# The last two layers of a fused two-network kernel: attention by head pairs with GEMMs between its tiles, norms from column sums, two products split into parts

## The chip, the cores and the metric
The kernel runs on one core of a Trainium2 chip. The metric is device time in microseconds (us) of one execution; lower is better. The engines are TensorE (PE; PEld is its weight load), VectorE (DVE), ScalarE (ACT), GpSimd (POOL) and SyncE (SP), which here only issues DMAs. They run at once and meet at semaphores; each takes its own instructions in order.

## The reference
The program computes two networks in a row on 512 tokens of width 1024. The first (two layers, mixer and mixture of experts) is not touched. The second, also two layers, is:

```python
def second_block(x, norm1_g, w_in, q_norm_g, k_norm_g, sg_norm_g, sg_w, sg_b, conv_w,
              w_out, norm2_g, ffn_w_up, ffn_conv_w, ffn_w_down):
    ...
    for l in range(DEPTH):                                   # DEPTH = 2
        h = _rmsnorm(x, norm1_g[l])
        p = h @ w_in[l]                                      # 1024 x 2048
        q, k, v, su, sv, cb, cc, cx = jnp.split(p, split_at, axis=-1)
        q = _axial_rope(_rmsnorm(q.reshape(b, s, 8, 64), q_norm_g[l]), tabs)
        k = _axial_rope(_rmsnorm(k.reshape(b, s, 2, 64), k_norm_g[l]), tabs)
        a_out = _block_attention(q, k, v.reshape(b, s, 2, 64))   # softmax, 4 query heads per key head
        g_out = _spatial_gating(su, sv, sg_norm_g[l], sg_w[l], sg_b[l])
        c_out = cb * _dwconv3(cc * cx, conv_w[l])
        mix = jnp.concatenate([a_out, g_out, c_out], axis=-1)
        x = x + mix @ w_out[l]                               # 1024 x 1024
        h2 = _rmsnorm(x, norm2_g[l])
        up = _dwconv3(h2 @ ffn_w_up[l], ffn_conv_w[l])       # 1024 x 5632
        gate, val = jnp.split(up, 2, axis=-1)
        x = x + (jax.nn.silu(gate) * val) @ ffn_w_down[l]    # 2816 x 1024
    return x
```

(In the quoted loop norm and rope of q and of k are drawn together into one line each.)

## The kernel before
Everything is fp32 and feature-major: a [128 features, 512 tokens] tile is one PSUM bank, and xT and hT hold eight of them. A "ticket" (TB, from order_b) is one tile that TensorE makes in one bank; tickets go round the eight banks in the order of the list, the second entry names the engine that frees the bank ("V" VectorE, "A" ScalarE), and TensorE opens a bank when the ticket eight places earlier is freed. So one list sets TensorE's order and the banks.

A product in fp32 streams its moving operand several times (two records a matmul in the trace). The gate, value and up products are instead "split": weights and rows are each a rounded high part in fp32r plus a low part, and a tile is the sum of three one-pass terms, high x high, low weights x high rows, high weights x low rows (of_parts, 24 matmuls of 512 columns for a contraction of 1024). The high part of a weight block is a ScalarE copy (high_part(n), into ring slot 4 or 5), the low part a POOL subtraction in place (low_part(n), L798), one block of 128x4096 ahead of TensorE. SP loads weight blocks into ring slots in the order of blocks_b; a block waits for the last reader of its slot. The output product (wo, 8 tiles, contraction 1024) and the second feed-forward product (dn, 8 tiles, contraction 2816 = 22 x 128) are plain fp32.

A layer: whole_norm("n1") squares x on ScalarE, sums with eight ones-matmuls 512 columns wide, so that the sum stands in all 128 partitions, takes a root (ScalarE) and a reciprocal (VectorE) over 128x512, scales xT into hT (L1808, one instruction per 128 features), and makes high (ScalarE) and low parts (L1812). Then the tiles q, kk, v, k, su, sv, cb, cc, cx, with a head norm of the same kind (nr, halves-matmul, root, reciprocal, L1826) for each of six q and k tiles, and rope (sw, swap-matmul, three VectorE instructions, L1831 to L1833). Then gating and convolution. Attention runs head by head over 8 heads x 4 query tiles: logits (L, a matmul with 64 rows), maximum and its negation (L1880, L1881), exponential with sum (L2212), reciprocal and multiplication (L1885, L1886), four transposes (T, L1320), copies to bwT (L1875 or L1915), and after four tiles the values (pv, four matmuls of 64 columns). Then wo, the second norm n2, 44 up tiles (ug, uv), and dn.

Line 819 is the helper mm, through which nearly every matmul goes; line 1915 is the ScalarE copy helper and 685 POOL's helper for small DMAs.

## Time and profile before

| | us |
|---|---|
| median of 3 runs | 3931.11 (3924.7 to 3931.31) |
| profiled execution | 3928.03 |
| its span | 3926.4 |
| mean granted TensorE clock | 0.917 of full |
| TensorE busy | 3308.7 |
| VectorE, ScalarE, POOL busy | 1194.5, 863.4, 669.9 |
| first network and set-up | 2449.6 |
| first layer of the second network | 734.0 |
| second layer and output | 742.8 |

Times in the trace count from the span's start. A busy figure is the sum of instruction records; TensorE's records overlap a little at their ends, so a stage that is full shows a busy time equal to its length. PEclk is the clock that the throttle granted TensorE: 1.0 is 2.4 GHz and 0.5 is 1.2 GHz. Stages are named A to G in the text: A first norm with its first two tiles, B the rest up to attention, C attention, D output product, E second norm with its first two tiles, F the other 42 up tiles, G second feed-forward product.

### The profile page before, as it was taken

The numbers are of one execution on the slowest core, as the hardware profiler recorded it, in microseconds if no ns is written. First come the engines' busy times: TensorE is split into PE (matmuls) and PEld (weight loads), VectorE is DVE, ScalarE is ACT, GpSimd is POOL, SyncE is SP. The second block draws the span as 40 slices with busy tenths as digits, with TensorE's granted clock in tenths as the row PEclk, the third lists the DMA queues.
The fourth block names the chain that finished last, engine by engine and source line by source line (L and its number), as shares of the span: only waits on it lengthen the run. The fifth ranks groups of instructions, "written<-read, shape, count | busy, mean of one in ns | idle before, by whom it ended". The sixth has DMA issues, their size and how long they took to land. (4 is left out here: it accounts for less than half of the span.)

```text
span 3926.4 us, 41122 instructions
## 1 busy us (share of the span) xinstructions
PE 3308.7 (84%) x14327; PEld 1938.3 (49%) x14327; DVE 1194.5 (30%) x2137; ACT 863.4 (22%) x1257; POOL 669.9 (17%) x360
## 2 busy tenths in 40 slices
PE   6976997888784985898888875889799989879999
PEld 4753564333322763564333332743587456338854
DVE  4564213111103465312211111452433016433310
ACT  4333111111112423201111111222332022323300
POOL 4220000111112311010111113200343030013300
PEclk8987997999996997898899997989899998889999
DMA  5124132999994114133899997110223311012322
GB/s 198 65 95 139 54 141 96 406 409 409 409 393 172 65 59 154 65 101 137 326 408 409 409 407 287 60 38 22 65 86 88 106 66 65 1 43 86 101 59 66
DMA packets 287657, 663.59 MB, mean 169 GB/s; under 512 B 20190, under 2 KB 110612, under 8 KB 287504
## 3 DMA queue, kind: packets, MB, share of 16 engines
q1 hardware_dynamic: 269632, 623.43, 42.8%
q0 software_dynamic: 17872, 38.14, 2.7%
q8 instruction: 93, 1.52, 0.2%
q14 instruction: 60, 0.49, 0.0%
HBM read 653.64 MB, written 25.69 MB: 173 GB/s over the span
## 5 line engine op out<-in xcount | busy, mean ns | idle before, releaser
L819 PE MATMUL psum<-s_parts 128*128 128x512 f32 (+3 forms) x3392 | 823.5, 396 | 114.5 <-ACT s_parts L1915 96.7
L819 PE MATMUL psum<-s_ring,s_units 128*64 128x512 f32 x3168 | 743.9, 619 | 135.6 <-DMA s_ring<-in_w_expert_in 96.5
L819 PEld LDWEIGHTS psum<-s_parts 128*128 128x128 f32 (+1 forms) x3392 | 632.6, 192 | 277.0 <-issue 103.2
L819 PEld LDWEIGHTS psum<-s_ring,s_units 128*64 128x64 f32 x3168 | 247.5, 141 | 588.3 <-issue 445.8
L819 PE MATMUL psum<-s_units,s_ring 128*128 128x512 f32 x1216 | 524.0, 592 | 3.3 <-DVE s_units L1588 3.3
L819 PE MATMUL psum<-s_units 128*128 (+9 forms) x1544 | 404.9, 441 | 111.3 <-ACT s_units L1915 51.3
L798 POOL TENSOR_TENSOR s_parts<-s_ring,s_parts 128x4096 fp32r<-128x4096 f32 x30 | 270.4, 9019 | 988.6 <-ACT s_parts L1915 988.6
L819 PEld LDWEIGHTS psum<-s_units,s_ring 128*128 128x128 f32 x1216 | 230.8, 190 | 290.9 <-issue 290.1
L819 PE MATMUL psum<-s_h_low,s_parts 128*128 128x512 f32 (+1 forms) x1440 | 355.7, 389 | 0.0
L819 PEld LDWEIGHTS psum<-s_units 64*128 64x128 f32 (+3 forms) x1544 | 207.2, 203 | 238.3 <-issue 188.9
L819 PEld LDWEIGHTS psum<-s_h_low,s_parts 128*128 128x128 f32 (+1 forms) x1440 | 269.0, 187 | 57.4
L707 POOL TENSOR_TENSOR s_parts<-s_ring,s_parts 128x4096 fp32r<-128x4096 f32 (+1 forms) x22 | 180.5, 8209 | 596.3 <-ACT s_parts L1915 596.3
L1704 DVE TENSOR_SCALAR s_put_at<-psum,s_half_row 128x1 int32<-128x1 f32 x66 | 14.4, 218 | 706.9 <-DMA ys_scratch<-s_units,s_put_at 706.9
L1915 ACT ACTIVATE s_parts<-s_ring 128x4096 fp32r<-128x4096 f32 (+1 forms) x52 | 181.3, 3493 | 197.2 <-DMA s_ring<-in_w_in 197.2
L1915 ACT ACTIVATE s_units<-psum 128x512 f32<-128x512 f32 (+1 forms) x246 | 143.2, 598 | 285.7 <-PE psum L819 236.9
L749 POOL DMA_INDIRECT s_units<-h_scratch,s_take_at x66 | 82.9, 1256 | 597.3 <-DVE s_take_at L1699 477.5
L1899 DVE SCALAR_TENSOR_TENSOR s_units<-psum,s_par,s_units 128x511 f32<-128x511 f32 x88 | 66.0, 750 | 301.2 <-ACT s_units L2239 301.2
L2239 ACT ACTIVATE s_units<-psum,s_par 128x512 f32<-128x512 f32 x88 | 60.8, 690 | 335.5 <-PE psum L819 335.5
L1398 DVE RECIPROCAL s_temps<-s_temps 128x512 f32<-128x512 f32 x36 | 120.7, 3353 | 25.1 <-ACT s_temps L1940 25.1
L2116 ACT ACTIVATE s_units<-psum,s_gsl 128x512 f32<-128x512 f32 x66 | 45.4, 687 | 358.7 <-PE psum L819 358.7
L758 POOL DMA_INDIRECT ys_scratch<-s_units,s_put_at x66 | 67.1, 1016 | 321.2 <-ACT s_units L2116 286.5
L819 PE MATMUL psum<-s_hT,s_ring 128*128 128x512 f32 x256 | 110.4, 593 | 1.7 <-ACT s_hT L1915 1.7
(306 smaller groups left out, 2407.1 us busy)
## 6 DMA issues: line engine op xcount, KB each, us to landing
s_ring<-in_w_expert_in SPq DMA_DIRECT2D x132, 2048.0 KB, 23.9
s_ring<-in_w_expert_out SPq DMA_DIRECT2D x66, 2048.0 KB, 24.9
s_ring<-in_w_in SPq DMA_DIRECT2D x28, 2048.0 KB, 8.0
s_ring<-in_w_ada SPq DMA_DIRECT2D x24, 2048.0 KB, 8.1
s_ring<-in_ffn_w_up SPq DMA_DIRECT2D x44, 1024.0 KB, 6.9
s_ring<-in_ffn_w_down SPq DMA_DIRECT2D x16, 1408.0 KB, 7.1
s_ring<-in_w_out SPq DMA_DIRECT2D x8, 2048.0 KB, 7.8
s_units<-ys_scratch POOLq DMA_DIRECT2D x16, 512.0 KB, 6.3
```

The source lines that it names most:

```text
L707: pool.tensor_tensor(parts[:, s, 0:size], ring[:, s, 0:size], parts[:, 4 + n % 2, 0:size].bitcast(F32), ALU.subtract).then_inc(weights_low ...
L749: pool.indirect_dma_start(out=xs[u % 2], out_offset=None, in_=h2_dram[:, :], in_offset=bass.IndirectOffsetOnAxis(ap=take_at[:, u % 2, 0:1] ...
L758: pool.indirect_dma_start(out=ys_dram[:, :], out_offset=bass.IndirectOffsetOnAxis(ap=put_at[:, u, 0:1], axis=0), in_=ys[u], in_offset=None ...
L798: pool.tensor_tensor(parts[:, RB.slot(SPLIT_B[n]), :], raw, parts[:, 4 + n % 2, :].bitcast(F32), ALU.subtract).then_inc(weights_low.sem, w ...
L819: return pe.matmul(o, lhsT=lhsT, rhs=rhs, start=start, stop=stop)
L1398: link(ve.reciprocal(T[:, 2, :], T[:, 3, :]))
L1704: ve.tensor_scalar(put_at[:, u % 2, :], psum[:, 7, 1:2], 2.0, half_row[:, 0:1], ALU.mult, ALU.add).then_inc(m_put_written.sem, m_put_writt ...
L1899: link(ve.scalar_tensor_tensor(out=up_t[:, b, 1:SEQ], in0=o[:, 0:SEQ - 1], scalar=w[0], in1=up_t[:, b, 1:SEQ], op0=ALU.mult, op1=ALU.add))
L1915: return ae.activation(o, i, ACT.Copy) if scale is None else ae.activation(o, i, ACT.Copy, scale=scale)
L2116: ae.activation(ys[u], psum[:, 5 + u, :], ACT.Copy, scale=gsl[:, u:u + 1]).then_inc(m_ys_made.sem, m_ys_made.more())
L2239: ae.activation(up_t[:, n % 4, :], o, ACT.Copy, scale=par[:, col:col + 1]).then_inc(up_centre.sem, up_centre.more())
```

## The change
Only the second network's layers change.

- Norms: eight tiles of squares are the stationary operands and one column of ones moves, so the sums of 512 tokens land in four columns. Root and reciprocal cover 128x4. Four (or, for head norms, eight) matmuls with the identity spread them over partitions again. Scaling reads the factor from PSUM. The first two tiles of GEMMs start on each high part as it is made (first_two). A head's factor of q goes into the exponential's scale, that of k is multiplied in.
- Order: kk, su, v come first. sv, cc, cx and cb leave the stage before attention and stand in pieces (FILL) between its steps, in bank 7; sv is made feature-major and transposed.
- Attention: one step is a query tile of two heads, logits from the two halves of the rows into two banks, one maximum over both. Weights are transposed unscaled, and the sums' reciprocals are applied once per head pair to the values' result.
- wo and dn are split like the rest. The mixed rows' parts take the place of h's, the hidden rows' high parts take three places. Weight blocks use three slots, and up's last two blocks are half as large. POOL makes the second weight block's low part ahead of six table loads.

```diff
-LINKS = {"A": 177, "B": 138}
+LINKS = {"A": 177, "B": 78}
...
+FILL = {0: (("cc", 0), 0, 3), 1: (("cx", 0), 0, 3), 2: (("sv", 0), 0, 2), 3: (("sv", 0), 2, 3), 4: (("sv", 1), 0, 2), 5: (("sv", 1), 2, 3),
+        6: (("cc", 1), 0, 2), 7: (("cc", 1), 2, 3), 8: (("cx", 1), 0, 2), 9: (("cx", 1), 2, 3), 10: (("cb", 0), 0, 2), 11: (("cb", 0), 2, 3),
+        12: (("cb", 1), 0, 2), 13: (("cb", 1), 2, 3)}
...
+UPS = [(2 * n, 2) for n in range(KF // 2 - 1)] + [(KF - 2, 1), (KF - 1, 1)]
...
 def blocks_b():
...
+    b = [(("in", 1), ("su", 1), 0), (("in", 0), ("q", 3), 1), (("in", 3), ("cx", 1), 2), (("in", 2), ("cb", 1), 0)]
+    b += [(("wo", 0), ("wo", 3), 1), (("wo", 1), ("wo", 7), 2)]
+    b += [(("up", n), ("uv", i + c - 1), n % 3) for n, (i, c) in enumerate(UPS)]
+    b += [(("dn", m), ("dn", m), s) for m, s in enumerate((0, 1, 2, 0, 1, 2, 1, 2))]
...
+            def first_two(names, w, cols, norm):
+
+                outs = [opened(name) for name in names]
+                for k in range(KD):
+                    pe.wait_ge(h_high_b.sem, h_high_b.at(l, KD * norm + k + 1))
+                    for o, c0 in zip(outs, cols):
+                        mm(o, w[0][:, k, c0:c0 + P], h_rows[0][k], k == 0, False)
+                for o, c0 in zip(outs, cols):
+                    term(o, w, c0, h_rows, 1)
+                pe.wait_ge(h_low_b.sem, h_low_b.at(l, KD * (norm + 1)))
+                for o, c0 in zip(outs, cols):
+                    done(term(o, w, c0, h_rows, 2))
+
+            def token_sums(name, squares, first):
                 o = opened(name)
                 for k in range(KD):
                     pe.wait_ge(x_squared_b.sem, x_squared_b.at(l, first + k + 1))
-                    last = mm(o, ones[:], squares[:, k, :], k == 0, k == KD - 1)
+                    for t in range(NT):
+                        last = mm(o[:, t:t + 1], squares[k][:, tok(t)], ones[:, 0:1], k == 0 and t == 0, k == KD - 1 and t == NT - 1)
                 done(last)
...
+            def spread(name, at, heads):
+
+                o = opened(name)
+                for t in range(NT):
+                    for c in range(heads):
+                        a, width = at + heads * t + c, P // heads
+                        last = mm(o[width * c:width * c + width, tok(t)], few[:, a:a + 1].to_broadcast([P, width]), ident[:], True, True)
+                done(last)
...
+            def rope_swap(x):
+                o = opened(("sw", x))
+                if x == 0:
+                    pe.wait_ge(tables_in.sem, tables_in.at(l, 9 * 16))
...
             for m in range(KD):
...
+                w = block_parts(("dn", m))
+                if m == 0:
+                    o = opened(("dn", 0))
+                    for k in range(KF):
+                        pe.wait_ge(hidden_low.sem, hidden_low.at(l, k + 1))
+                        for x, (a, b) in enumerate(TERMS):
+                            last = mm(o, w[a][:, k, :], hid_rows[b][k], k == 0 and x == 0, k == KF - 1 and x == 2)
+                    done(last)
+                else:
+                    fm_parts(("dn", m), w, 0, hid_rows)
...
+                    ve.wait_ge(TB.done.sem, TB.done_at(l, ("L", j, 1)))
+                    link(ve.tensor_reduce(few[:, 152 + b:154 + b], psum[:, b:b + 2, :], AX_X, ALU.max))
+                    r = 120 + 8 * i + 2 * t
+                    ve.scalar_tensor_tensor(out=few[:, 156 + b:158 + b], in0=few[:, 152 + b:154 + b], scalar=-1.0, in1=few[:, r:r + 2],
+                                            op0=ALU.mult, op1=ALU.mult).then_inc(max_negated_b.sem, max_negated_b.more())
...
+                if j == 10:
+                    high_part(4)
...
+            for k in range(6, KF):
+                high_hidden(k)
+                if k == 11:
+                    high_part(19)
+            for n in range(20, len(SPLIT_B)):
+                high_part(n)
```

How TensorE's order stands in attention before: rows are line, operation, output and inputs, size, and how many in a row. Logits of one tile (L819, 128x512) alternate with the four transposes of the tile two earlier (L1320), and after four tiles come the values (64x512):

```order
L819 MATMUL psum<-s_units 128x512
L1206 REGISTER_ALU
L1318 REGISTER_ALU
L1320 MATMUL psum<-s_ident,s_units 128x128 x4
L1206 REGISTER_ALU
L1325 REGISTER_ALU
L1326 REGISTER_ALU
L819 MATMUL psum<-s_units 64x512 x4
```

The same place now, steps 2 and 3 (L861 is mm, L1394 the transposes). Each step has two logit matmuls, two or one terms of a split tile (s_parts x16, s_h_low x8) and two groups of transposes:

```order
L861 MATMUL psum<-s_units 128x512 x2
...
L861 MATMUL psum<-s_parts 128x512 x16
...
L1394 MATMUL psum<-s_ident,s_units 128x128 x4
...
L1394 MATMUL psum<-s_ident,s_units 128x128 x4
...
L861 MATMUL psum<-s_units 128x512 x2
L861 MATMUL psum<-s_h_low,s_parts 128x512 x8
```

GEMM pieces moved from ahead of attention to between logits and transposes.

POOL at the start of a layer before: both weight subtractions stand ahead of all table loads.

```order
L798 TENSOR_TENSOR s_parts<-s_ring,s_parts 128x4096 [waits b_weights_high]
L796 REGISTER_ALU
L798 TENSOR_TENSOR s_parts<-s_ring,s_parts 128x4096 [waits b_weights_high]
L803 ISA
L685 DMA s_units<-in_rope 128x512 [waits b_freed_by_vector]
L685 DMA s_units<-in_rope 128x512
L685 DMA s_units<-in_swap 128x128
```

POOL at the same place now:

```order
L839 TENSOR_TENSOR s_parts<-s_ring,s_parts 128x4096 [waits b_weights_high]
L844 ISA
L726 DMA s_aT<-in_swap 128x128 [waits b_freed_by_vector]
L726 DMA s_units<-in_rope 128x512 x2
L837 REGISTER_ALU
L839 TENSOR_TENSOR s_parts<-s_ring,s_parts 128x4096 [waits b_weights_high]
L726 ISA
L726 DMA s_aT<-in_sg_w 128x4x128
L726 ISA
L726 DMA s_units<-in_sg_b 64x128
```

The second subtraction moved between the rope tables and the gating tables.

TensorE at the first norm now: sums with one moving column, the spread, then two tiles at once, then the third tile.

```order
L861 MATMUL psum<-s_ones,s_temps 128x1 x4
L1327 ISA
L861 MATMUL psum<-s_ident,s_lamv 128x128 x4
L1257 ISA
L861 MATMUL psum<-s_parts 128x512 x32
L861 MATMUL psum<-s_h_low,s_parts 128x512 x16
L861 MATMUL psum<-s_parts 128x512 x16
```

Before, eight matmuls of 512 moving columns stood there, and the first tile's 24 matmuls came alone behind all high parts.

## Rows read from the trace of the kernel before

**Rows 1.** Page, part 1: busy us, share of the span, instructions of TensorE.

```profile
PE 3308.7 (84%) x14327; PEld 1938.3 (49%) x14327; DVE 1194.5 (30%) x2137; ACT 863.4 (22%) x1257; POOL 669.9 (17%) x360
```

**Rows 2.** Stage table, A to G: window, length, busy by engine, clock, DMA share, GB/s.

```profile
2449.60:2481.80 32.20, 21.19 (x64) 13.89 (x65) 14.65 (x21) 11.13 (x18) 13.11 (x10) 0.80 0.11 35
2481.80:2583.60 101.80, 95.29 (x493) 77.18 (x492) 47.77 (x45) 24.55 (x40) 17.95 (x2) 0.99 0.24 83
2583.60:2706.70 123.10, 103.63 (x288) 39.62 (x288) 61.55 (x156) 38.80 (x89) 0.00 (x0) 0.81 0.00 1
2706.70:2761.80 55.10, 55.05 (x129) 24.44 (x130) 4.85 (x7) 4.41 (x7) 0.00 (x0) 1.00 0.12 38
2761.80:2803.10 41.30, 19.46 (x66) 13.02 (x65) 25.00 (x21) 15.28 (x14) 18.11 (x2) 0.75 0.16 51
2803.10:3031.60 228.50, 228.50 (x1010) 189.27 (x1009) 83.24 (x105) 72.96 (x73) 86.39 (x19) 1.00 0.26 81
3031.60:3183.60 152.00, 151.19 (x353) 66.65 (x351) 7.72 (x11) 12.23 (x12) 17.67 (x2) 1.00 0.34 95
3183.60:3215.10 31.50, 20.43 (x66) 13.84 (x67) 14.79 (x21) 8.13 (x12) 5.08 (x9) 0.78 0.31 103
...
3495.60:3536.90 41.30, 19.47 (x65) 13.04 (x64) 25.00 (x21) 15.28 (x14) 18.11 (x2) 0.75 0.15 51
```

**Rows 3.** Timeline: start, length, engine, line, operation, [idle before, releaser].

```profile
352.94 1.13 PE L819 MATMUL psum<-s_units 64*128 64x512 f32 x4
...
354.00 0.66 PE L1055 MATMUL psum<-s_ident,s_units 128*128 128x128 f32 x4
354.58 0.30 PEld L819 LDWEIGHTS psum<-s_units 64*128 64x128 f32 x4 [0.17 <-issue]
...
636.92 13.84 PE L819 MATMUL psum<-s_ring,s_hT 128*128 128x36 f32 x64 [11.43 <-ACT s_hT L1945]
...
2508.91 1.94 PE L819 MATMUL psum<-s_temps,s_ident 128*64 128x512 f32 x8
```

**Rows 4.** Stage table, two microseconds within the narrow matmuls.

```profile
638.00:640.00 2.00, 2.00 (x11) 2.00 (x11) 0.00 (x0) 0.07 (x1) 0.00 (x0) 0.50 0.00 0
```

**Rows 5.** Timeline, first norm of the first layer.

```profile
2458.12 0.69 DVE L1801 TENSOR_SCALAR s_temps<-psum 128x512 f32<-128x512 f32 x1 [8.09 <-PE psum L819]
...
2462.90 5.39 DVE L1808 SCALAR_TENSOR_TENSOR s_hT<-s_xT,s_par,s_temps 128x512 f32<-128x512 f32 x8
...
2468.20 4.90 DVE L1812 TENSOR_TENSOR s_h_low<-s_hT,s_parts 128x512 fp32r<-128x512 f32 x8
```

**Rows 6.** Timeline, VectorE beside POOL subtractions.

```profile
2536.38 9.01 POOL L798 TENSOR_TENSOR s_parts<-s_ring,s_parts 128x4096 fp32r<-128x4096 f32 x1 [30.23 <-ACT s_parts L1915]
...
2541.75 4.20 DVE L1826 SCALAR_TENSOR_TENSOR s_units<-s_units,s_sc,s_temps 128x512 f32<-128x512 f32 x1
...
2767.03 18.11 POOL L798 TENSOR_TENSOR s_parts<-s_ring,s_parts 128x4096 fp32r<-128x4096 f32 x2 [221.63 <-ACT s_parts L1915]
...
2775.72 13.95 DVE L1808 SCALAR_TENSOR_TENSOR s_hT<-s_xT,s_par,s_temps 128x512 f32<-128x512 f32 x8
```

**Rows 7.** Groups by line (busy us, mean ns | idle before), then DMA issues (KB, us to landing).

```profile
L798 POOL TENSOR_TENSOR s_parts<-s_ring,s_parts 128x4096 fp32r<-128x4096 f32 x29 | 261.4, 9019 | 988.6 <-ACT s_parts L1915 988.6
...
L1915 ACT ACTIVATE s_parts<-s_ring 128x4096 fp32r<-128x4096 f32 x28 | 101.1, 3617 | 109.4 <-DMA s_ring<-in_w_in 109.4
...
L2212 ACT ACTIVATE s_units<-psum,s_sc 128x512 f32<-128x512 f32 x64 | 44.0, 688 | 84.2 <-DVE s_sc L1881 84.2
L1880 DVE TENSOR_REDUCE s_sc<-psum 128x1 f32<-128x512 f32 x64 | 43.9, 686 | 100.1 <-PE psum L819 100.1
...
L2212 ACT ACTIVATION_READ_ACCUMULATOR s_units<-psum,s_sc 128x1 f32 x64 | 12.3, 193 | 0.0
...
s_ring<-in_ffn_w_down SPq DMA_DIRECT2D x16, 1408.0 KB, 7.1
...
s_units<-in_sg_norm_g POOLq DMA_DIRECT2D x2, 128.0 KB, 5.2
```

More of the change, by code:

```diff
@@ L410, in counts @@
     def counts(order, who):
-        return sum(w == who for _, w in order)
+        return sum(w == who for _, w, *_ in order)
     def sig(name, per, credit=0):
@@ L1210, in done @@
                 last.then_inc(TB.done.sem, TB.done.more())
-            def fm(name, w, c0, rhs, kn):
-                o = opened(name)
-                for k in range(kn):
-                    last = mm(o, w[:, k, c0:c0 + P], rhs[:, k, :], k == 0, k == kn - 1)
-                done(last)
             def block_parts(name):
@@ L2147, in high_part @@
+                last = {name: last for name, last, *_ in RB.blocks}[SPLIT_B[n - 2]]
                 if n >= 2:
-                    last = {name: last for name, last, *_ in RB.blocks}[SPLIT_B[n - 2]]
                     ae.wait_ge(TB.done.sem, TB.done_at(l, last))
                 else:
-                    ae.wait_ge(TB.done.sem, l * TB.done.per + (TB.index[RB.reader_last(4 + n)] + 1))
-                copy(parts[:, 4 + n % 2, :], ring[:, RB.slot(SPLIT_B[n]), :]).then_inc(weights_high.sem, weights_high.more())
@@ L2156, in h_high_part @@
-            def h_high_part():
-                first = h_high_b.given
+                    ae.wait_ge(TB.done.sem, l * TB.done.per + (TB.index[last] + 1))
+                copy(parts[:, 4 + n % 2, 0:size], ring[:, s, 0:size]).then_inc(weights_high.sem, weights_high.more())
+            def h_high_part(which):
                 for k in range(KD):
-                    ae.wait_ge(h_made_b.sem, h_made_b.at(l, first + k + 1))
+                    if k < KD - 1:
+                        ae.wait_ge(h_made_b.sem, h_made_b.at(l, (KD - 1) * which + k + 1))
+                    else:
+                        ae.wait_ge(TB.by(("nb", which)).sem, TB.freed_at(l, ("nb", which)))
@@ L2230, in _ @@
+            starts = {i: n for n, (i, _) in enumerate(UPS)}
             for i in range(KF):
-                if i % 2 == 0 and 2 <= i < KF - 2:
-                    high_part(4 + i // 2 + 1)
+                if i in starts and starts[i]:
+                    high_part(7 + starts[i])
                 for c, kind in enumerate(("ug", "uv")):
```

691 lines of the change are left out of this document (400 added, 291 removed).

## The prediction

> **What bounds the kernel now.** I read the page's busy line first: TensorE is busy 84% of the span, far above the others [rows 1]. Then I cut the last part of the span into its two layers and each layer into stages with the stage table [rows 2]. The reader should see three kinds of stage. In the gate and value products, the output product and both feed-forward products TensorE is full at full clock, so time there is its own work. At each of the four whole-row norms it stands idle and restarts on the 1.2 GHz level (granted 0.75 to 0.80). In attention (123.1 us a layer) the granted clock is 0.81 and VectorE and ScalarE are busy 61.6 and 38.8 us: nobody is full, tiles wait for each other. The change acts on this part alone, about 734 us for each of two layers; the first 2449.6 us are untouched.
>
> **Prices.** A split product of a 128x512 tile with contraction 1024 (24 one-pass matmuls) takes 228.5 / 42 = 5.44 us, from stage F, which holds 42 such tiles back to back [rows 2]. A plain fp32 matmul of 512 columns takes 55.1 / 64 = 0.86 us (stage D). So a contraction step of 128 costs 0.86 plain and 0.68 split. Two 64-row matmuls in different row groups run side by side: the pair starts at 352.94 and its successor at 354.00, 1.06 us; four transposes are followed after 0.58 us. Four 64-column matmuls in column pairs take 1.94 us, so 0.43 to 0.49 each [rows 3]. Sixty-four records with 36 moving columns took 13.84 us, 0.22 each [rows 3], while the clock stayed at its 1.2 GHz level though the records filled the time [rows 4]; I take 0.11 each at 2.4 GHz.
>
> **The change, part by part (one layer).**
>
> *Norm from column sums (stages A and E).* Before, sums end, then TENSOR_SCALAR, root and a reciprocal over 512 columns: 4.8 us from 2458.12 to 2462.90, then 5.39 us of scaling; the low parts end at 2473.1 [rows 5]. After, the wide sum is 32 matmuls with one moving column (64 records), 7.0 us at full clock and 13.8 us at half. Narrow work did not raise the clock in [rows 3, 4]; whether it holds a high one no row shows. So I take half clock throughout for the first norm, which starts after idle time, and for the other three, which start behind full GEMMs, the middle of both ends: 10.5 us. Root and reciprocal then cover 4 columns, about 0.8 us in all; spreading them costs 8 records, 1.7 us at half clock. Scaling starts at 13.2 us, runs 5.6 us, and two GEMMs now start on each part as it comes. Their first term runs on half clock until the clock rises (7 us), the second takes 3.6, the low parts 4.9 us behind the scaling, the third term 3.6. Two tiles are done 28.6 us after the start (32 for the first norm), against 32.2, 31.5 and twice 41.3 [rows 2].
> The 41.3 of the second norms has a cause of its own: two POOL subtractions (18.11 us) run beside the scaling, which takes 13.95 us instead of 5.39 [rows 6]. One instruction slips between them and the next waits for the second's end. After, this scaling reads PSUM and one SBUF operand, like the DVE groups that are not slowed, and the POOL work stands earlier. The Trainium skill (SBUF — State Buffer, section "Who interferes with whom") says that a DVE instruction with two SBUF inputs is blocked for the whole length of a GpSimd instruction that reads SBUF. By that rule, the trace agrees: the single instruction at 2541.75 takes 4.20 us and ends at 2545.95, just behind the POOL subtraction (2536.38 + 9.01 = 2545.39).
> Sum: first layer A 0, second A −2.9, E −12.7 in both.
>
> *From there to attention (stage B, 101.8 us).* Eight of fourteen tiles' worth of products leave for attention. What stays: six tiles 32.6; five narrow head sums with five swaps 9.3; value transposes, key copies and the spread 3.8; 45.7 in all. VectorE loses six reciprocals over 512 columns, which were beside TensorE's work and save nothing. The change adds a wait: the first rope swap on TensorE waits for nine table loads, and six of these are now issued by POOL behind the second weight subtraction. That one starts after ScalarE's copy (3.6 us) behind the norm, takes 9.0, then 3.5 us of issues and 5.2 until the last lands [rows 7]: about 43 and 40 us from the start of the layers, where TensorE arrives at 38.4 and 35. Behind it TensorE's own queue stands (su, q). Cost 4.4 and 5.4 us; I add 2 for hand-overs. After: 52 and 53 us, a saving of 49.
>
> *Attention (stage C, 123.1 us).* TensorE's work after: 16 logit pairs 17.0; 32 groups of four transposes 18.6; 32 value matmuls in column pairs 13.8; eight tiles moved here 43.5; gating weights, transposes, gating product and four spreads 7.1; 100.0 us. Beside it per step ScalarE has two exponentials of 0.69 with accumulator reads of 0.19 (1.7) and a copy (0.6), VectorE a maximum over two banks and a copy (0.7) [rows 7]. The maximum of two banks is not in the trace: one takes 0.69, so 0.69 to 1.37, I take 1.25, nearest to twice. That makes 2.3 and 2.1 us against TensorE steps of 3.8 to 10 us, so TensorE is the bound. What it does not cover: the last five steps have no GEMM, the chain maximum, exponential, transpose, copy, values, scaling costs 6.4 us beyond its work. ScalarE's weight copy in step 10 and bank 7's hand-overs 3. POOL's subtraction behind step 10 (9.0 us) locks out the convolution and the negated maximum, which have two SBUF inputs: VectorE comes free 8 us late, of which the next steps absorb some; 5 us. After: 114.4, a saving of 8.7. The range of the tail and waits together is 0 to 30.
>
> *Output product (D, 55.1 us)*: 64 steps of contraction at 0.68: 43.6, a saving of 11.5. Its second weight block costs ScalarE 3.6 and POOL 9.0 after attention, hidden by 21.8 us of the first four tiles. The first tile takes its parts in the order in which they come, 4.8 us of work, which hides the last head's 3 us chain.
>
> *Second feed-forward (G, 152.0 us)*: 176 steps at 0.68: 119.7. The first tile waits for sixteen low parts of the hidden rows, 0.61 us each, made only after the last up product, with a POOL subtraction (0.69 of 9.0, so 6.2 us) locking VectorE out in the middle: 21.3 us instead of 15. Weight blocks share three slots now. Block 6 loads after block 4: 7.1 + 2.5 + 6.2 us and hand-overs against 15 us of block 5, so 1 to 2 us of stall. After: 128.5, a saving of 23.5. F stays: same 42 tiles, its added copies are beside TensorE.
>
> Sum: first layer 0 + 49.7 + 8.7 + 11.5 + 12.7 + 23.5 = 106; second 2.9 + 48.6 + 8.7 + 11.5 + 12.7 + 23.5 = 108. 3928.0 − 214 = 3714 us for the profiled execution, whose span is 3926.4; the median of the runs lies 3.1 above it, so 3717, rounded **3715**.
>
> One rule bears on D and G. The Trainium skill (TensorE: Matmul & The Clock Gate, section "Back-to-back issue gap") gives N / 2.4 + 2.5 ns, 0.216 us for 512 columns. Stage F shows 0.227. By the rule, 240 steps would cost 155 instead of 163 us a layer, and the sum would be some 16 us lower. The measured tile decides.
>
> **Rivals.**
> 1. *Attention stays a chain.* The GEMMs add to the steps instead of filling them. One step's chain is 1.06 + 1.25 + 1.7 + 0.6 + 0.7, 5.3 us; 16 of them plus moved tiles and values (57) are 142 and the tail 8: 150 us. Against 114.4 that is +71 in two layers: **3786**. For it: 0.81 of clock and idle engines now. Against it: two logit pairs are in flight and each step has 1.8 to 5.4 us of GEMM before the transposes of two steps earlier.
> 2. *Clock and lock cost nothing.* The narrow sums run at full clock (−3.5 to −6.8 a norm, and the first terms 3.6 faster), the table wait and POOL's lock are absorbed: about −45: **3670**. Against it are [rows 4, 6].
> 3. *Half clock stays in attention*: tiles cost nearly twice; +86 a layer: **3886**. Against: stage F is at 1.00 right behind stage E's 0.75, so dense GEMMs regain the clock, and no step of the first fourteen is without them [rows 2].
> 4. *Slower than before: weight parts become serial.* If each down block's load, copy, subtraction and product do not overlap (7.1 + 2.5 + 6.2 + 15), eight cost 246 us instead of 128.5, +118 a layer: 3950. It decides from a period of 29 us a block; three slots and two part buffers speak against it.
>
> **How the numbers follow.** Forecast 0.68; rival 1 0.13; rival 2 0.13; rival 3 0.04; rival 4 0.01; the rest 0.01 for no change. The range takes in rivals 1 and 2 and the 0 to 30 us of attention: 3660 to 3795. A measurement tells about 0.2% (8 us) from no change. Faster 0.97, same 0.01, slower 0.02.
>
> **What would show it.** The last stage table should read about 29 to 32, 52, 114, 44, 29, 228, 128 us a layer. Right: transposes in attention seldom wait, and the granted clock there is above 0.9; a TensorE wait of 4 to 5 us before the first swap, ended by a table load; the narrow sums at half clock; the DVE low parts of the hidden rows split by a POOL subtraction. Wrong: attention above 130 us with gaps before transposes; down blocks far from 15 us apart; scaling in the second norm still slowed.

## The result, and the profile after

The changed kernel takes **3768.96 us** (median; 3762.38 to 3771.59). Beside it the kernel before took 3930.55 (3924.7 to 3931.31): a ratio of 0.9589, 95% interval 0.9573 to 0.9606. The forecast was 3715 with a range of 3660 to 3795, so the sign and the range held, but the gain is 162 us where the forecast stood for 216. The rest of this document is mostly about those 54 us.

The busy line of the page, part 1, answers to [rows 1]. TensorE lost 135 us of busy time and stayed at the same share, because the span shrank with it:

```profile
PE 3173.7 (84%) x15027; PEld 2050.9 (54%) x15027; DVE 1138.5 (30%) x2001; ACT 946.6 (25%) x1337; POOL 807.7 (21%) x382
```

The stage table of the changed kernel, cut at the same seams as [rows 2]: stages A to G of the first layer, then A, C and G of the second. Columns are the window, its length, busy time and instructions of the five engines (TensorE's matmuls, its weight loads, VectorE, ScalarE, GpSimd), the granted clock, DMA share, GB/s.

```profile
2448.10:2480.10 32.00, 29.48 (x122) 26.51 (x123) 11.07 (x22) 15.50 (x21) 6.86 (x5) 0.63 0.07 20
2480.10:2533.06 52.96, 47.96 (x224) 36.21 (x223) 11.01 (x24) 13.63 (x21) 16.79 (x8) 0.94 0.25 83
2533.06:2672.39 139.33, 108.91 (x556) 70.58 (x556) 68.00 (x85) 55.78 (x114) 17.72 (x2) 0.90 0.10 33
2672.39:2716.09 43.70, 43.70 (x194) 36.16 (x193) 6.22 (x9) 12.10 (x10) 18.06 (x2) 1.00 0.15 49
2716.09:2743.00 26.91, 24.54 (x122) 21.74 (x121) 12.07 (x21) 11.38 (x13) 4.95 (x1) 0.75 0.24 79
2743.00:2971.48 228.48, 228.48 (x1010) 189.25 (x1009) 89.73 (x112) 78.61 (x81) 92.25 (x12) 1.00 0.28 87
2971.48:3101.50 130.02, 123.05 (x529) 100.42 (x527) 22.41 (x26) 34.60 (x33) 57.75 (x18) 0.97 0.35 100
3101.50:3133.00 31.50, 26.56 (x122) 23.90 (x123) 11.75 (x22) 11.87 (x14) 5.92 (x4) 0.73 0.26 88
...
3185.80:3328.08 142.28, 112.99 (x557) 72.06 (x557) 67.97 (x85) 55.78 (x114) 17.72 (x2) 0.88 0.10 33
...
3627.20:3757.07 129.87, 122.75 (x529) 100.26 (x527) 22.42 (x26) 27.33 (x25) 43.70 (x7) 0.97 0.25 67
```

Set beside the forecast (us, first layer):

| stage | before | forecast | after |
|---|---|---|---|
| A first norm, two tiles | 32.2 | 32 | 32.0 |
| B head products, rope | 101.8 | 52 | 53.0 |
| C attention with the gate GEMMs | 123.1 | 114.4 | 139.3 |
| D output product | 55.1 | 43.6 | 43.7 |
| E second norm, two tiles | 41.3 | 28.6 | 26.9 |
| F up products | 228.5 | 228.5 | 228.5 |
| G down product | 152.0 | 128.5 | 130.0 |

One row is far off: C, by 24.9 us in the first layer and 27.9 in the second, 52.8 of the 54 us. C took in eight tiles, 43.5 us of GEMMs, and grew by 16 us, where the forecast had it shrink by 9.

What C consists of now. TensorE is busy 108.9 us and idle 30.4. The gaps, from TensorE's timeline of the changed kernel (start, length, line, operation, count, then in brackets the idle time before and what ended it):

```profile
2546.70 5.51 PE L861 MATMUL psum<-s_parts 128*128 128x512 f32 x16 [5.78 <-ACT s_units L2050]
2565.57 3.94 PE L861 MATMUL psum<-s_parts 128*128 128x512 f32 x16 [0.27 <-ACT s_units L2050]
2577.58 5.26 PE L861 MATMUL psum<-s_units 128*64 128x512 f32 x16 [2.12 <-ACT s_units L2050]
2589.34 1.09 PE L861 MATMUL psum<-s_ident,s_lamv 128*64 128x128 f32 x16 [1.77 <-ACT s_units L2050]
...
2632.76 6.77 PE L861 MATMUL psum<-s_parts 128*128 128x512 f32 x16 [9.09 <-ACT s_units L2050]
...
2662.30 3.94 PE L1394 MATMUL psum<-s_ident,s_units 128*128 128x128 f32 x16 [4.83 <-ACT s_units L2050]
```

Two gaps are large, 5.78 and 9.09 us, and the same sixteen matmuls that take 3.94 us elsewhere take 5.51 and 6.77 behind them: the granted clock was 0.50 from 2546 to 2550 and from 2632 to 2638. Each of these two gaps is ended by a ScalarE copy (line 2050 is its copy helper) from the one bank in which the gate GEMMs are made. What held ScalarE stands in the timeline of all engines, first around step 0, then around step 11:

```profile
2535.57 8.91 POOL L839 TENSOR_TENSOR s_parts<-s_ring,s_parts 128x4096 fp32r<-128x4096 f32 x1 [22.14 <-ACT s_parts L2050]
2536.12 8.37 DVE L1959 SCALAR_TENSOR_TENSOR s_lamv<-s_lamv 128x2 f32<-128x2 f32 x1
...
2544.53 0.78 ACT L2351 ACTIVATE s_units<-psum,s_lamv 128x512 f32<-128x512 f32 x1 [7.84 <-DVE s_lamv L1959]
...
2546.05 0.59 ACT L2050 ACTIVATE s_units<-psum 128x512 f32<-128x512 f32 x1
```

```profile
2621.65 8.81 POOL L839 TENSOR_TENSOR s_parts<-s_ring,s_parts 128x4096 fp32r<-128x4096 f32 x1 [77.17 <-ACT s_parts L2050]
2622.40 8.07 DVE L1959 SCALAR_TENSOR_TENSOR s_lamv<-s_lamv 128x2 f32<-128x2 f32 x1
2630.59 0.78 ACT L2351 ACTIVATE s_units<-psum,s_lamv 128x512 f32<-128x512 f32 x1 [9.12 <-DVE s_lamv L1959]
...
2632.11 1.08 ACT L2050 ACTIVATE s_units<-psum 128x512 f32<-128x512 f32 x2
```

Line 1959 multiplies two maxima by two scale factors and by −1, four numbers a partition. Elsewhere it takes 0.16 us; beside a GpSimd subtraction of a weight block it ends when that ends (2535.57 + 8.91 = 2544.48). The exponentials (line 2351) wait for it, and in ScalarE's order the copy of the GEMM's bank stands behind the exponentials. TensorE, which needs neither maximum nor exponential for its next GEMM, waits for the bank.

So the reading before any experiment: stage C is 100.0 (work at full clock, as forecast) + 8.9 (busy time above that, put down to half clock) + 14.9 (two lock gaps) + 9.2 (eight shorter hand-overs, 0.27 to 2.12 us, all ended by ScalarE) + 6.3 (tail) = 139.3. Of the 8.9, 7.9 can be read off: four groups of sixteen matmuls took 1.57, 2.83, 1.61 and 1.87 us longer than their like at full clock. The last us is not placed.

### The profile page after: what moved, and what is told of

Its sections match the earlier page's. It is cut to its first block and busy times, and to the rows that moved or that the text cites. A ratio compares the mean times of both kernels' runs of the same rounds, so it can differ in the third digit from the quotient of the medians.

```text
span 3766.8 us, 42402 instructions
## 1 busy us (share of the span) xinstructions
PE 3173.7 (84%) x15027; PEld 2050.9 (54%) x15027; DVE 1138.5 (30%) x2001; ACT 946.6 (25%) x1337; POOL 807.7 (21%) x382
## 3 DMA queue, kind: packets, MB, share of 16 engines
q8 instruction: 98, 1.61, 0.2%
## 5 line engine op out<-in xcount | busy, mean ns | idle before, releaser
L861 PE MATMUL psum<-s_parts 128*128 128x512 f32 (+1 forms) x3744 | 951.9, 406 | 84.0 <-ACT s_units L2050 37.7
L861 PEld LDWEIGHTS psum<-s_parts 128*128 128x128 f32 (+1 forms) x3744 | 723.1, 194 | 279.3 <-ACT s_units L2050 46.0
L861 PE MATMUL psum<-s_ring,s_units 128*64 128x512 f32 x3168 | 742.5, 617 | 135.2 <-DMA s_ring<-in_w_expert_in 96.1
L839 POOL TENSOR_TENSOR s_parts<-s_ring,s_parts 128x4096 fp32r<-128x4096 f32 (+2 forms) x52 | 407.9, 7843 | 875.4 <-ACT s_parts L2050 875.4
L861 PEld LDWEIGHTS psum<-s_ring,s_units 128*64 128x64 f32 x3168 | 247.2, 141 | 587.0 <-issue 446.8
L861 PE MATMUL psum<-s_h_low,s_parts 128*128 128x512 f32 (+1 forms) x1872 | 469.8, 391 | 11.2 <-DVE s_hid_low L2021 11.2
L861 PEld LDWEIGHTS psum<-s_h_low,s_parts 128*128 128x128 f32 (+1 forms) x1872 | 350.0, 188 | 95.1 <-DVE s_hid_low L2021 12.1
L861 PE MATMUL psum<-s_units 128*128 (+9 forms) x1520 | 303.6, 420 | 81.8 <-ACT s_units L2050 31.4
L2050 ACT ACTIVATE s_parts<-s_ring 128x4096 fp32r<-128x4096 f32 (+3 forms) x74 | 237.3, 3210 | 254.6 <-PE psum L861 103.5
L861 PEld LDWEIGHTS psum<-s_units 64*128 64x128 f32 (+3 forms) x1520 | 177.8, 196 | 163.5 <-issue 109.1
L1810 DVE TENSOR_SCALAR s_put_at<-psum,s_half_row 128x1 int32<-128x1 f32 x66 | 14.4, 218 | 702.9 <-DMA ys_scratch<-s_units,s_put_at 702.9
L861 PE MATMUL psum<-s_units,s_ring 128*128 128x512 f32 x512 | 221.5, 592 | 3.3 <-DVE s_units L1694 3.3
L861 PEld LDWEIGHTS psum<-s_units,s_ring 128*128 128x128 f32 x512 | 97.1, 190 | 123.3 <-issue 122.7
```

Of the source, the lines that this page charges most:

```text
L839: pool.tensor_tensor(parts[:, s, 0:size], ring[:, s, 0:size], parts[:, 4 + n % 2, 0:size].bitcast(F32), ALU.subtract).then_inc(weights_low ...
L861: return pe.matmul(o, lhsT=lhsT, rhs=rhs, start=start, stop=stop)
L2050: return ae.activation(o, i, ACT.Copy) if scale is None else ae.activation(o, i, ACT.Copy, scale=scale)
```

## The experiments

The diffs are shortened: "..." and the comments in them stand for code left out.

**1. Does the blocked maximum hold TensorE?** The operation with two tensors in SBUF becomes two with one each:

```diff
-ve.scalar_tensor_tensor(out=few[:, 156 + b:158 + b], in0=few[:, 152 + b:154 + b], scalar=-1.0, in1=few[:, r:r + 2],
-                        op0=ALU.mult, op1=ALU.mult).then_inc(...)
+ve.tensor_scalar(few[:, 156 + b:157 + b], few[:, 152 + b:153 + b], few[:, r:r + 1], -1.0, ALU.mult, ALU.mult)
+ve.tensor_scalar(few[:, 157 + b:158 + b], few[:, 153 + b:154 + b], few[:, r + 1:r + 2], -1.0, ALU.mult, ALU.mult).then_inc(...)
```

> The negated maximum, one VectorE operation with two tensors in SBUF, becomes two tensor_scalar operations with one tensor each (the second factor is the per-partition scalar); nothing else changes, and VectorE issues 16 operations more a layer. Theory L (the blocked negated maximum held the exponentials, these ScalarE's copy of the GEMM bank, and this TensorE): the 8.37 and 8.07 us operations go to about 0.2 us each although the POOL subtraction beside them still runs 8.9 us, the TensorE gaps of 5.78 and 9.09 us go, with them part of the 8.9 (first layer) and 13 us (second) that half clock costs in attention; attention about 119 us instead of 139.3, time 3729 us (3722 to 3740). Rival B (any small VectorE operation in SBUF is blocked beside POOL): 3769 within 3. Rival Q (ScalarE's own 3.6 us weight copy and the table load of 1.28 us ahead of the exponentials are what holds them): gaps shrink to 3 to 5 us, time 3745 to 3760.

Measured 3736.35 us, ratio 0.951 (0.9494 to 0.9526): 33 us less than the changed kernel. Timeline and stage table of this run:

```profile
2532.93 9.02 POOL L839 TENSOR_TENSOR s_parts<-s_ring,s_parts 128x4096 fp32r<-128x4096 f32 x1 [22.13 <-ACT s_parts L2050]
2533.49 0.21 DVE L1959 TENSOR_SCALAR s_lamv<-s_lamv 128x1 f32<-128x1 f32 x1
...
2611.83 8.92 POOL L839 TENSOR_TENSOR s_parts<-s_ring,s_parts 128x4096 fp32r<-128x4096 f32 x1 [69.88 <-ACT s_parts L2050]
2612.59 0.21 DVE L1959 TENSOR_SCALAR s_lamv<-s_lamv 128x1 f32<-128x1 f32 x1
...
2612.84 0.68 DVE L1977 COPY s_units<-psum 128x512 f32<-128x512 f32 x1
2613.44 7.60 DVE L2005 TENSOR_SCALAR s_temps<-s_units,s_par 128x512 f32<-128x512 f32 x1
...
2530.43:2655.59 125.16, 104.74 (x556) 67.40 (x557) 61.38 (x101) 55.95 (x114) 17.94 (x2) 0.96 0.11 37
```

Both subtractions still run 9 us and the negated maximum takes 0.21 us beside them. Attention falls from 139.3 to 125.2 us. The 5.78 us gap is gone; of the 9.09 us some 4 stay, in two waits of 1.37 and 2.45, since the next VectorE operation in the row, the convolution's first, is now the blocked one (7.60 us, 0.47 when alone). That is why it is 125 and not the 119 that I expected. Rivals B and Q fall.

**2. The lock made shorter.** GpSimd's two subtractions beside attention in four pieces each:

```diff
-pool.tensor_tensor(parts[:, s, 0:size], ring[:, s, 0:size], parts[:, 4 + n % 2, 0:size].bitcast(F32), ALU.subtract).then_inc(...)
+pieces = 4 if n in (3, 4) else 1
+for c in range(pieces):
+    part = slice(size // pieces * c, size // pieces * (c + 1))
+    last = pool.tensor_tensor(parts[:, s, part], ring[:, s, part], parts[:, 4 + n % 2, part].bitcast(F32), ALU.subtract)
+last.then_inc(...)
```

> The two POOL subtractions that run beside attention (low parts of the 4th and 5th weight block) are issued as four of 1024 columns each instead of one of 4096; same work, same order. Theory L, with VectorE let in between two pieces: its blocked operation takes at most 2.3 us, the gaps of 5.78 and 9.09 us go to 0 to 1.5 us, time 3731 us (3724 to 3745). Rival B2 (the next piece is at the port before VectorE is, so the four act as one): 3769 within 3.

Measured 3738.48 us, ratio 0.9515 (0.9499 to 0.9531). Timeline rows of GpSimd and VectorE in this run, with the stage row of its attention:

```profile
2533.54 9.44 POOL L842 TENSOR_TENSOR s_parts<-s_ring,s_parts 128x1024 fp32r<-128x1024 f32 x4 [22.13 <-ACT s_parts L2053]
...
2534.10 1.86 DVE L1962 SCALAR_TENSOR_TENSOR s_lamv<-s_lamv 128x2 f32<-128x2 f32 x1
...
2531.03:2656.27 125.24, 108.04 (x556) 69.23 (x557) 60.76 (x85) 56.01 (x114) 19.40 (x8) 0.93 0.11 37
```

Same code on VectorE, same work on GpSimd, and the blocked operation ends with the first piece instead of the fourth. VectorE gets in between pieces. The 5.78 us gap is gone and the 9.09 is 2.62. Rival B2 falls. Two different mends of the lock bring 33 and 30 us, so the lock's length was in the chain of cause. That both give 125.2 us in attention is in part chance: here TensorE is idle for 17.2 us at clock 0.93, with the one-input maximum for 20.4 at 0.96.

**3. Or is it the order on ScalarE?** The blocked maximum is left as it is; within a step, what ScalarE takes from PSUM stands ahead of the two exponentials:

```diff
 for j in range(PAIRS + 3):
+    if values_of(j) is not None:
+        take(("pv", values_of(j)), ...)
+    for name in filled(j): ...                  # take the GEMM's bank
+    if 2 <= j < PAIRS + 2: copy(bwT[0] ...)     # turned first head of step j - 2
     if j < PAIRS:
         ae.wait_ge(max_negated_b.sem, ...)
         for c in range(2): ae.activation(bp[...], psum[...], ACT.Exp, ...)
-    (the same takes, here)
```

The order in which ScalarE's releases are counted moves with it.

> ScalarE's order inside a step of attention: what it takes from PSUM for TensorE (values, a GEMM's bank, the turned first head of two steps before) goes ahead of the two exponentials instead of behind them. The negated maximum stays blocked 8.4 and 8.1 us. Theory O (the exponentials have two steps of slack, the takes have none, so it is the order on ScalarE that turns the lock into TensorE's idle time and makes the 1.77 us before each spread and the 2.12, 0.90 and 0.36 us before the values): all of 5.78 + 9.09 and about 8 of the 9.2 us of hand-overs go, and the half clock behind them; attention 139.3 to about 110 us, time 3711 us (3703 to 3725). Rival L-only (the blocked maximum holds TensorE by the transposes too, which need the exponentials two steps on): only the hand-overs go, 3769 - 2 x 9 = 3751 (3745 to 3757).

Measured 3717.73 us, ratio 0.9462 (0.9446 to 0.9478): 51 us less than the changed kernel, within 7 of what I had expected, and more than either mend of the lock. From its timeline and stage table:

```profile
2534.45 8.47 DVE L1965 SCALAR_TENSOR_TENSOR s_lamv<-s_lamv 128x2 f32<-128x2 f32 x1
...
2606.32 9.40 DVE L2013 SCALAR_TENSOR_TENSOR s_temps<-s_units,s_par,s_temps 128x511 f32<-128x511 f32 x1
...
2531.39:2646.55 115.16, 104.85 (x556) 66.62 (x556) 68.43 (x85) 56.39 (x114) 17.97 (x2) 0.96 0.12 41
```

VectorE is blocked as long as ever, 8.47 and 9.40 us. Only the first of these is the negated maximum, so the clean test is step 0: maximum blocked, gap of 5.78 gone. At the second subtraction the maximum had slipped through before it, and the operation held is the convolution's last. Attention takes 115.2 us, 0.8 from the forecast's 114.4. The waits of 1.77 us before each spread and of 0.27 to 2.12 us elsewhere went along with the gap of 5.78; around the second subtraction 4.7 us are left where the 9.09 stood, in waits of 1.13, 2.12 and 1.49. The exponentials have two steps before anyone needs them, the takes have none. So the chain of cause is: the lock delays a thing that has slack, and the order on ScalarE hands that delay to things that have none. The lock's length was foreseen; what it would hold, through ScalarE's queue, was not.

**4. What the GEMMs between the tiles are worth.** The same eight GEMMs, pairs and copies, but the GEMMs ahead of step 0.

```diff
-FILL = {0: (("cc", 0), 0, 3), 1: (("cx", 0), 0, 3), 2: (("sv", 0), 0, 2), 3: (("sv", 0), 2, 3), ...}
+FILL = {-8: (("cc", 0), 0, 3), -7: (("cx", 0), 0, 3), -6: (("cc", 1), 0, 3), ..., -1: (("cb", 1), 0, 3)}
-for j in range(PAIRS + 3):
+for j in range(-8, PAIRS + 3):
```

> The eight gate GEMMs (43.5 us of TensorE a layer) are issued ahead of the first attention step, in two banks by turns, instead of between its tiles; the pair tiles, the order of everything else and all work stay. Theory F (between tiles the GEMMs cover the chain through VectorE and ScalarE and keep the clock up): attention alone runs with gaps at half clock, about 6.4 us a step of 16, 4 x 7.3 for the values, 4 x 3 for spreads and hand-overs, so about 144 + 43.5 = 187 us instead of 139.3 a layer: time 3864 us (3830 to 3880). Rival P (the pairs alone made the gain, a step is bound by ScalarE's 2.6 us or TensorE's 3.2 us at full clock): 16 x 3.5 + 4 x 5 + 4 x 2.5 + 6 = 92 + 43.5 = 135.5 a layer: 3761 us (3745 to 3775).

Measured 3773.88 us, ratio 0.9602 (0.9586 to 0.9618): 5 us slower than the changed kernel, in the rival's range and far from the theory's 3864. The intervals of the two kernels overlap, but the traces have the same sign: stages A to C of the first layer take 227.0 us here and 224.3 there. I had the bare chain far too slow: its stage row, from the first logits on, stands below, and the same row of the next experiment further down.

```profile
2576.68:2676.66 99.98, 67.37 (x365) 35.28 (x364) 56.21 (x80) 50.83 (x108) 8.81 (x1) 0.85 0.07 22
```

So of what B and C gained together (224.9 to 192.3 us in the first layer) the placement of the GEMMs accounts for 2.5 us a layer. The rest, 30 us a layer, lies with the pairs, the narrow head norms and the smaller work on VectorE; no run takes these apart, so the larger part of the gain in B and C has no cause shown. The run also moves more than the GEMMs: GpSimd's subtraction for the fourth weight block now runs beside them, and attention has one subtraction beside it (8.81 us, x1) where the changed kernel has two (17.72, x2). Rival P gave as its reason that the pairs alone keep TensorE going. The next run tests that reason.

> The run with ScalarE's takes ahead of the exponentials (3717.7 us), and on top of it the eight gate GEMMs ahead of attention, as in the run that gave 3773.9. Theory X (the GEMMs between the tiles brought little in the changed kernel because ScalarE's order let the copy of their one bank, and with it TensorE, wait for the exponentials; with that order mended they cover the chain): attention with its GEMMs 115 us between the tiles, 43.5 + 80 = 123.5 ahead of them, so 3734 us (3728 to 3745), 16 slower than 3717.7. Rival Y (GEMMs between tiles bring nothing, a step of a pair alone keeps TensorE as busy): 3713 to 3722.

Experiments 3 and 4 in one kernel: 3745.44 us, ratio 0.9529 (0.9514 to 0.9543).

```profile
2576.60:2663.92 87.32, 68.26 (x366) 34.99 (x365) 56.89 (x80) 51.22 (x108) 8.84 (x1) 0.82 0.08 25
```

| us | takes behind exponentials | takes ahead of them |
|---|---|---|
| GEMMs ahead of attention | 3773.9 | 3745.4 |
| GEMMs between the tiles | 3769.0 | 3717.7 |

With the old order the placement is worth 5 us, with the new one 28. Rival Y falls: the pairs alone do not keep TensorE busy; the bare chain takes 87.3 us with 68.3 busy at clock 0.82, where with the GEMMs between them the same steps take 115.2 − 43.5 = 71.7. Theory X has the direction, but I took 80 us for that chain, so the price came out as 28 and not 16. In the changed kernel the interleaving was there, and most of its gain was eaten by ScalarE's takes behind the exponentials. Of the 23 us between the 28 and the 5, an estimate puts some 16 on the subtraction at step 0, which only the kernels with the GEMMs between the tiles have there: its gap and the slower matmuls behind it are 5.78 + 1.57 us in the first layer and 5.77 + 2.79 in the second. With the new order the same subtraction leaves no gap. A run in which the copy of the GEMM's bank alone moves was not made.

**5. The table wait.** The low part moves behind the gating loads in GpSimd's program:

```diff
 small(tables_in, cos_t, inp["rope"][0])
-low_part(1)
 small(tables_in, wsr, ...)
 ...
 small(tables_in, gvb, inp["sg_norm_g_2"][l].partition_broadcast(P))
+low_part(1)
```

> GpSimd issues the six gating loads (weights, four bias rows, gains) ahead of its second low part instead of behind it. Theory T (the first rope swap waits 4.22 and 4.80 us for the last of these loads, which could only be issued once that subtraction was done): both waits go, 3769 - 9 = 3760 us (3757 to 3763). Rival T2 (the six issues now delay the low part, and the first input block waits for it instead): between 3766 and 3778.

Measured 3755.55 us, ratio 0.9551 (0.9536 to 0.9566), 13 us less, more than the 9 of the two waits and just under the range that I gave. The changed kernel's swap and the GEMM behind it first, then this run's issue of the last table and the same two, without a wait:

```profile
2490.74 2.07 PE L861 MATMUL psum<-s_temps,s_aT 128*128 128x512 f32 x2 [4.22 <-DMA s_units<-in_sg_norm_g]
2491.83 5.99 PE L861 MATMUL psum<-s_parts 128*128 128x512 f32 x16
```

```profile
2455.43 0.58 POOL L726 DMA_DIRECT2D s_units<-in_sg_norm_g  x1
...
2488.38 1.10 PE L861 MATMUL psum<-s_temps,s_aT 128*128 128x512 f32 x2
2488.92 4.24 PE L861 MATMUL psum<-s_parts 128*128 128x512 f32 x16
```

The swap went from 2.07 to 1.10 us and the sixteen matmuls behind it from 5.99 to 4.24; in the second layer they went from 2.07 to 1.10 and from 5.25 to 4.24. With the waits of 4.22 and 4.80 that is 13.7 us: behind each wait TensorE had also run at half clock.

**6. The first block of the down product.** Blocks 1 to 7 take the low weights' term last and wait for it only then; GpSimd makes block 1's low part when VectorE's low hidden parts are through:

```diff
-w = block_parts(("dn", m))
+w = block_parts(("dn", m), m == 0)     # without the wait for the low part
-fm_parts(("dn", m), w, 0, hid_rows)
+for a, b in ((0, 0), (0, 1), (1, 0)):
+    if a: block_parts(("dn", m))
+    for k in range(KF): mm(o, w[a][:, k, :], hid_rows[b][k], ...)
 ...
+if n == 19: pool.wait_ge(hidden_low.sem, hidden_low.at(l, KF))
```

> Second feed-forward product: blocks 1 to 7 take their terms in the order high x high, high x low of the hidden values, low of the weights x high, and wait for the low part of the weights only before the last; GpSimd makes the low part of block 1 only when VectorE has made all low hidden parts. Same work. Theory H (the 5.6 us stall in block 0 and the half clock behind it are the POOL subtraction that blocks VectorE's low hidden parts; block 6 waits 1.4 us for a low part that its last third alone needs): block 0 takes 15 us instead of 23.2, the wait of block 6 goes, 9.5 us a layer: 3750 us (3746 to 3756). Rival H2 (VectorE, at 0.62 us a part against TensorE's 0.68, can't keep up anyway, or block 1 now waits for its low part): 3758 to 3769.

Measured 3750.78 us, ratio 0.954 (0.9525 to 0.9555), 18 us less. Block 0 of the changed kernel, with the blocked operation and TensorE behind it, then of this run:

```profile
2978.64 6.17 POOL L839 TENSOR_TENSOR s_parts<-s_ring,s_parts 128x2816 fp32r<-128x2816 f32 x1 [7.74 <-ACT s_parts L2050]
2979.01 6.95 DVE L2021 TENSOR_TENSOR s_hid_low<-s_units,s_h_low 128x512 fp32r<-128x512 f32 x2 [0.74 <-ACT s_h_low L2050]
...
2985.41 1.22 PE L861 MATMUL psum<-s_h_low,s_parts 128*128 128x512 f32 x2 [5.61 <-DVE s_hid_low L2021]
...
2971.48:2994.72 23.24, 17.63 (x68) 14.03 (x67) 17.56 (x19) 11.98 (x19) 6.17 (x1) 0.85 0.24 63
```

```profile
2989.36 6.28 POOL L841 TENSOR_TENSOR s_parts<-s_ring,s_parts 128x2816 fp32r<-128x2816 f32 x1 [14.39 <-DVE s_hid_low L2030]
...
2975.55:2990.79 15.24, 15.24 (x67) 12.31 (x66) 11.91 (x19) 11.99 (x19) 1.43 (x1) 1.00 0.36 96
```

The subtraction moved out of the way, block 0 takes 15.2 us at clock 1.00 instead of 23.2 at 0.85, and block 1 is not held by its later low part. Block 6 no longer waits (1.35 us before). That is 9.4 us a layer, as theory H has it.

**7. What the split down product brings.** Undone alone: weights and hidden rows as plain fp32.

```diff
-w = block_parts(("dn", m))
-... three terms of high and low parts
+pe.wait_ge(weights_in_b[RB.slot(("dn", m))], RB.landed(l, ("dn", m), ("up",)))
+for k in range(KF): mm(o, wview(RB, ("dn", m), KF, P)[:, k, :], hid[:, k, :], k == 0, k == KF - 1)
```

> The changed kernel with its second feed-forward product as it was before: weights as they land and hidden rows in plain fp32, 22 steps of contraction a block; no high or low parts of either. Three ring slots as in the change. Theory S (the split product brings stage G what the forecast gave it, 0.18 us a step, less the stall in its first block): 176 steps of 0.86 are 151.4 us instead of 130.0, +21 a layer: 3811 us (3805 to 3816). Rival R (with the copies of ScalarE and the subtractions of POOL gone, stage F or the waits for loads change too, or three slots alone set stage G's length): outside 3800 to 3820.

Measured 3804.93 us, ratio 0.9683 (0.9667 to 0.97), 36 us slower than the changed kernel. Stage G of the first layer:

```profile
2970.03:3120.90 150.87, 150.87 (x353) 66.69 (x351) 7.03 (x10) 8.57 (x10) 8.85 (x1) 1.00 0.30 86
```

150.9 against 130.0: 20.9 us, as theory S has it. The total lies 6 us below its 3811, on the lower edge of its range. Twice 20.9 is 42, of which 6 do not show in the total. In this run the second layer's stages A and B take 82.9 us instead of 84.3 (its sums start without the wait of 1.78 us, and the swap waits 3.66 instead of 4.80), and its attention 140.2 instead of 142.3. Its two lock gaps are 4.22 and 7.54 instead of 5.77 and 9.09, but that by itself saved nothing: just ahead of each the same logits and weight terms took 1.6 us longer, and the gap ended with the subtraction as before. The other 2 to 3 us lie within the spread of the runs.

**8. All mends together**, with two more for what was left: the second channel's convolution in step 13 instead of 11, away from GpSimd's subtraction, and the first output product begun inside attention's tail.

```diff
+def wo_first(first, last): ...   # contraction steps first..last of output product 0
 for j in range(PAIRS + 3):
+    if j == PAIRS + 1: wo_first(0, 2)      # ahead of the last transposes
 ...
+    if j == PAIRS + 2: wo_first(2, 4)      # ahead of the last values; (4, 6) ahead of the last spread
-if j in (4, 11):
+if j in (4, 13):
```

> All mends together: ScalarE's takes ahead of the exponentials; negated maximum in two one-input operations; gating loads ahead of the low part; down product as in the run beside; the second channel's convolution in step 13 instead of 11, away from the POOL subtraction; the first output product taken in four pieces (two of its eight contraction steps each) in front of the last transposes, the last values, the last spread and behind it. If the costs add: 3717.7 - 9 (tables) - 19 (down product) - 8 (what is left of the lock in steps 10 to 12) - 8 (5.6 us of waits in the tail a layer, of which 4 are covered) = 3674 us (3665 to 3690). Rival: the waits left over overlap, so that each mend beside the order brings half: 3696.

Measured **3673.93 us**, ratio 0.9348 (0.9335 to 0.9361): the sum of 3674 that I had given comes out, and this version beats both kernels, the changed one by 95 us. Experiments 3, 5 and 6 measured 51 + 13 + 18 = 83 us apart; the one-input maximum, the convolution's move and the tail bring the other 12 together, and were not told apart. The sum comes out, though not term by term: the tables and the down product brought 31 us where I had 28, these three 12 where I had 16. The busy line and the attention row, which now holds 4.1 us of the output product (six contraction steps of 0.68) besides:

```profile
PE 3154.4 (86%) x15027; PEld 2039.6 (56%) x15027; DVE 1103.2 (30%) x2033; ACT 947.7 (26%) x1337; POOL 807.1 (22%) x382
...
2530.19:2643.23 113.04, 107.48 (x577) 70.11 (x578) 57.62 (x103) 57.80 (x116) 17.98 (x2) 0.98 0.12 41
```

## Why the prediction was right or wrong

**Prices, D and F: right.** D took 43.7 against 43.6 us for 64 split steps; the back-to-back tile kept its 5.44 us. The down product's split was worth 20.9 us of stage time (experiment 7) where the sum had 23.5.

**The norms: right for the first, off both ways in the others.** A took 32.0 as forecast. In E the two GpSimd subtractions are gone from beside the scaling and it takes 5.35 us; the narrow sums took 9.35 us where I took the middle of both ends, 10.5. So E took 26.9 us, 1.7 less than forecast. How much of the 14.4 us saved there each of the three brought (narrower sums, scaling from PSUM, no subtraction beside it), no run tells. A of the second layer was forecast at 28.6 and took 31.5, the same as before, so the 2.9 us that I had counted there did not come: its sums started 2.9 us behind the last block (a wait of 1.78 us in it) and took 11.6 us, since the clock fell about 2 us into them (in E about 5), and the next two terms gave some back, 9.0 us where I had 10.6. These misses cancel in the total.

**Stage B: right.** The added wait came as worked out, 4.22 us (forecast 4.4) in the first layer and 4.80 (5.4) in the second, ended by the load of the gains, and experiment 5 removes it. The half clock behind it, 4.7 us in both layers, had no term of its own; the 2 us that I added for hand-overs made up for most of it.

**Attention: the step that failed.** TensorE's 100.0 us of work at full clock held within 1 us (108.9 busy less the 7.9 read off above), and so did the tail (6.3 us, forecast 6.4). Three terms were too small. *Hand-overs*, 3 us for ScalarE's weight copy and bank 7: they are 9.2. Bank 7 has only 0.6 of them; 5.3 stand before three spreads and 3.4 before values, and for these I had no term. *The lock*, "5 us" for step 10: it is 9.09, and I counted only one of two locks. The fourth weight block's subtraction starts 2.5 us into attention (2535.57), on step 0, and I had no term for it: another 5.78. *The clock*: I counted TensorE's work at full clock; half clock behind the gaps makes it up to 8.9 dearer. Together 6.2 + 9.9 + 8.9 = 25.0 of the 24.9 us by which C was missed.
The sentence behind the second is the one that failed: VectorE "comes free 8 us late, of which the next steps absorb some". VectorE was indeed late by 8 us, and the next steps could have absorbed it all, as step 0 in experiment 3 shows. I had asked how late VectorE would be, and not who stands behind the operation that waits for it on the next engine. Line 2351 ahead of the copy in ScalarE's program could be read in the code.
The range of 0 to 30 us that I gave to tail and waits together was exceeded by little: they are 30.4 us, and the half clock 8.9 more. The total stayed inside 3660 to 3795 because that range also took in rival 1's 3786, and rival 1's mechanism did not occur.

**Stage G: right, a little low.** Block 0 took 23.2 instead of 21.3 us, since the clock fell in the stall; block 6 stalled 1.35 us of the "1 to 2". The terms that I gave for G add up to 127 to 128 us and not to the 128.5 that I put into the sum.

**Rivals.** Rival 1 named 3786 and its sign, attention above 130 us with gaps, came true, but not its mechanism: the gaps stand before GEMMs and spreads and are ScalarE's order, not a chain of a pair's steps. Without GEMMs between them (experiment 4 with the new order) the bare chain takes 87 us with values and tail inside it, where rival 1 had 85 us for sixteen steps of 5.3 and put both on top: a step is shorter than I had it, too. Rival 2 did not occur either: the first norm's sums ran at half clock, and neither the table wait nor the lock was absorbed. That the kernel with all mends comes out at 3674, beside its 3670, is chance: there the sums of the first norm still run at half clock (6.98 and 6.96 us), and what was mended is largely ScalarE's order and the down product, which rival 2 does not name. Rivals 3 and 4 did not occur.

## What to carry to other kernels

When an engine's instruction will be late, read the next engine's program from the instruction that waits for it: everything behind it inherits the delay, slack or none. Put what another engine is waiting for (a bank to be emptied) ahead of what has steps of slack, and only then weigh how long a lock lasts. And judge interleaving only with that order right: the same placement of eight GEMMs was worth 5 us with one order and 28 with the other. And when work is moved, look what else moves with it on the other engines: here a subtraction changed sides with the GEMMs.

## What the hardware showed that I had not expected

*How small a locked-out operation can be.* An operation on 128x2 elements took 8.37 us beside a GpSimd subtraction and 0.16 without. With one SBUF input, 128x1 took 0.21 us beside it, 128x512 took 7.60 (0.47 alone), and a copy from PSUM beside the same subtraction took its usual 0.68 (experiment 1). That size would not help I had priced in; that an operation with one input can be locked out I had not. The Trainium skill (VectorE: DVE Perf Modes, section "What auto-detection actually checks") lets an operation with a single source and its destination in SBUF use both ports if the outermost dimensions larger than one are even or equal; the 512 columns that were locked out meet that condition. Of an operand with no dimension larger than one the sentence says nothing; the trace has 0.21 us for it.

*The clock under narrow matmuls.* In the run with the plain down product the second layer's norm starts right behind dense work:

```profile
3122.33 3.87 PE L861 MATMUL psum<-s_ones,s_units 128*128 128x1 f32 x32
3126.06 6.96 PE L861 MATMUL psum<-s_ones,s_temps 128*128 128x1 f32 x32
```

Thirty-two records take 3.87 us, the next thirty-two, alike, 6.96: full clock first (0.12 us each), then the 1.2 GHz level (0.22), though TensorE never stood idle in between. The granted clock is 1.00 up to 3124, 0.94 up to 3126 and 0.50 from there on. One-column matmuls did not hold the clock that they found, which [rows 4] left open.
